# Token-side norm weights and wide splits of the turned banks in a four-layer float32 transformer on one Trainium2 core

## The reference, cut to what matters

```python
# first block, per layer
y = hybrid_mixer(x, ...)                       # in-projections, attention, gating, pooling, w_o
x = layer_norm(DN_ALPHA * x + y, ln1_g, ln1_b)
y = conv_gated_ffn(x, ...)                     # up, causal conv, silu gate, down
x = layer_norm(DN_ALPHA * x + y, ln2_g, ln2_b)
# second block, per layer
h = rmsnorm(x, norm_mix);  x = x + mixer2(h)   # delta rule, sparse attention, memory attention
h = rmsnorm(x, norm_ffn);  x = x + ffn2(h)
# at the end
return rmsnorm(x, norm_final)

layer_norm: (x - mean) * rsqrt(var + 1e-5) * g + b
rmsnorm:     x * rsqrt(mean(x * x) + 1e-6) * g
```

## Time and profile before

| | us |
|---|---|
| median of 3 runs | 2336.72 (2335.99 to 2337.41) |
| the profiled execution, its own time | 2335.5 |
| its span in the trace | 2333.4 |
| PE busy | 2182.3 (94%) |
| POOL busy | 1499.0 (64%) |
| ACT busy | 1072.1 (46%) |
| DVE busy | 938.7 (40%) |
| mean granted clock of PE | 0.961 of full |

### The profile page before, as it was taken

One profiled execution on the slowest core, in us unless ns is written; L12 is line 12 of the kernel. 1 busy time (PEld: TensorE's weight loads), 2 busy tenths in 40 slices (PEclk: granted clock), 3 DMA queues, 4 the chain that ended last, 5 costly groups with the idle time before them and its releaser, 6 DMA issues.

```text
span 2333.4 us, 35994 instructions
## 1 busy us (share of the span) xinstructions
PE 2182.3 (94%) x15336; PEld 2016.4 (86%) x15336; DVE 938.7 (40%) x1512; ACT 1072.1 (46%) x1511; POOL 1499.0 (64%) x632
## 2 busy tenths in 40 slices
PE   8999989899978989989999899899899899998997
PEld 7789977799868979879999899888789799998997
DVE  4342356422376546374112311456364561123113
ACT  4555555455545352345444444562522454544443
POOL 6688877698844233356778688662333566787885
PEclk9989999999979989999999999999989999999999
DMA  8345534355523122234445455342222344454553
GB/s 334 140 145 186 191 119 164 108 199 181 182 91 127 55 73 75 89 129 143 159 154 191 147 186 191 130 145 73 73 73 73 109 149 159 145 182 161 181 182 116
DMA packets 47183, 333.05 MB, mean 143 GB/s; under 512 B 5168, under 2 KB 5552, under 8 KB 7856
## 3 DMA queue, kind: packets, MB, share of 16 engines
q1 hardware_dynamic: 47024, 330.76, 41.0%
HBM read 329.69 MB, written 1.05 MB: 142 GB/s over the span
## 4 chain that ended last, share of the span: by engine, by line
PE 60%; DVE 8%; ACT 3%; issue 2%; POOL 0%; ACTq 0%; DVEq 0%
PE bank L146 14%; PE bank L148 13%; PE bank L147 13%; PE y L146 2%; PE y L148 2%; PE y L147 2%; PE bank L1679 2%; PE bank L1689 1%; DVE conv L1325 1%; PE bank L1612 1%; PE bank L1688 1%; DVE sc L2288 1%; PE bank L1734 1%; PE bank L1731 1%; PE bank L1507 1%
## 5 line engine op out<-in xcount | busy, mean ns | idle before, releaser
L336 POOL TENSOR_TENSOR w_lo<-w_raw,w_hi 128x1024 fp32r<-128x1024 f32 x602 | 1465.4, 2439 | 809.6 <-ACT w_hi L327 809.4
L327 ACT ACTIVATE w_hi<-w_raw 128x1024 fp32r<-128x1024 f32 x602 | 636.3, 1059 | 1055.5 <-PE bank L148 885.2
L146 PE MATMUL bank<-x_hi,w_hi 128*128 128x256 f32 x2960 | 881.0, 298 | 30.4 <-POOL w_lo L336 19.2
L147 PE MATMUL bank<-x_lo,w_hi 128*128 128x256 f32 x2960 | 851.8, 288 | 0.0
L148 PE MATMUL bank<-x_hi,w_lo 128*128 128x256 f32 x2960 | 851.6, 288 | 0.0
L146 PEld LDWEIGHTS bank<-x_hi,w_hi 128*128 128x128 f32 x2960 | 582.0, 197 | 57.1 <-issue 25.9
L147 PEld LDWEIGHTS bank<-x_lo,w_hi 128*128 128x128 f32 x2960 | 582.3, 197 | 10.6 <-issue 8.6
L148 PEld LDWEIGHTS bank<-x_hi,w_lo 128*128 128x128 f32 x2960 | 582.0, 197 | 0.0
L862 DVE SCALAR_TENSOR_TENSOR conv<-bank,par_sb,conv 128x254 f32<-128x254 f32 (+1 forms) x176 | 76.8, 478 | 255.0 <-ACT conv L850 253.5
L1188 DVE TENSOR_TENSOR hid_lo<-hid,hid_hi 128x512 fp32r<-128x512 f32 x22 | 44.8, 2038 | 246.7 <-ACT hid_hi L1183 246.7
L146 PE MATMUL y<-w_hi,hid_hi 128*128 128x512 f32 x352 | 139.2, 396 | 1.0 <-DVE hid_lo L884 1.0
...
## 6 DMA issues: line engine op xcount, KB each, us to landing
...
```

Source lines behind the costliest of these rows:

```text
L146: pe.matmul(out, lhs[0], rhs[0], start=start, stop=False, skip_group_check=skip)
L147: pe.matmul(out, lhs[0], rhs[1], start=False, stop=False, skip_group_check=skip)
L327: act.activation(self.hi[:, h % HALVES, :], self.raw[:, n % RAWS, i * HW:(i + 1) * HW], ACT.Copy).then_inc(*sig.up("high", h))
L336: pool.tensor_tensor(self.lo[:, h % HALVES, :], self.raw[:, n % RAWS, i * HW:(i + 1) * HW], self.hi[:, h % HALVES, :].bitcast(F32), ALU.su ...
```

## The change

It changes how the norms are computed and where their pieces stand in the queues.

- `Norm1` works in place on x_tok with the rows of weight and bias: `centred` = (x - mean) * weight, `scaled` = that * (1/sd) + bias, two scalar_tensor_tensor instructions with both tensor inputs in SBUF, instead of xn. For (0,1) ACT writes (x - mean)/sd and POOL applies the rows. PE turns x_tok itself, in the order (0,0), (1,0), (0,1), (1,1). The token copy needs no more work on POOL.
- A turned bank is split wide: ACT copies 128x512 from PSUM to x_hi (`high_parts`), DVE subtracts (`low_part`, 128x512).
- `Norm2` takes the squares' sums on ACT (Square with an accumulator), adds two 128x1 numbers on DVE, and writes xn = x_tok * (1/rms) * weight row in one instruction. Token tile 0 goes through to its end before tile 1's residual. The weight rows are loaded by five DMAs. The second `ln2` is folded into the first `norm_mix`.
- ACT's root of token tile 0 and the table load stand ahead of the weight halves +2 to +4, no longer behind them; POOL's queue follows.
- The feed-forward stages start in banks 4 and 5 instead of 0 and 1, and end in down8, down9, down10 behind val10.
- `Stream.by_tokens` and the branches on `self.split` are new, but nothing calls `by_tokens`, so the halves ahead of a norm are multiplied in the order of before.

```diff
 class Norm1:
     def pe(self, pe):
         net.main.pe(pe, self.end())
-        for tt in range(TT):
-            for k in range(KD):
-                if k % 4 == 0:
-                    pe.wait_ge(*sig.at("xn", *k_l, tt, k // 4))
+        for tt, half in ((0, 0), (1, 0), (0, 1), (1, 1)):
+            pe.wait_ge(*(sig.at("x_rest", *k_l) if (tt, half) == (0, 1) else sig.at("x_new", *k_l, tt, half)))
+            for k in range(4 * half, 4 * half + 4):
                 mm = pe.transpose(...)
     def act(self, act):
-        net.main.act(act, self.end())
...
+        main.act(act, self.end() - 6)
+        act.preload_act_table_set("sqrt_and_others")
+        root(0)
+        act.wait_ge(*sig.at("inverse", *k_l))
+        act.activation(net.xn[:, 0, HALF:D], net.xtok[:, 0, HALF:D], ACT.Identity, scale=net.rs[:, 0:1], bias=net.sd[:, 0:1]
+                       ).then_inc(*sig.up("xn_second", *k_l))
+        main.act(act, self.end())
+        root(1)
+        high_parts(net, act, k_l, self.tb)
     def dve(self, dve):
...
+        statistics(0)
+        dve.wait_ge(*sig.at("ln_rows_" + self.key, self.l))
+        centred(0, 0)
+        inverse(0)
...
+        scaled(0, 0)
+        statistics(1)
+        centred(1, 0)
+        inverse(1)
+        scaled(1, 0)
+        centred(1, 1)
+        low_part(net, dve, k_l, self.tb, 0)
+        scaled(1, 1)
+        for i in (1, 2, 3):
+            low_part(net, dve, k_l, self.tb, i)
     def pool(self, pool):
+        net.main.pool(pool, self.end() - 6)
...
+        net.pool_chain.step(pool.tensor_tensor(net.xtok[:, 0, c], net.xn[:, 0, c], rows[:, 0, c], ALU.mult))
+        pool.tensor_tensor(net.xtok[:, 0, c], net.xtok[:, 0, c], rows[:, 1, c], ALU.add).then_inc(*sig.up("x_rest", *k_l))
         net.main.pool(pool, self.end())

+def high_parts(net, act, k_l, tb):
+    for i in range(4):
+        act.wait_ge(*net.sig.at("turned_x", *k_l, i))
+        act.activation(net.xs[0][:, 2 * i:2 * i + 2, :], tb[i][:, :].rearrange("p (k t) -> p k t", k=2), ACT.Copy
+                       ).then_inc(*net.sig.up("x_turned_high", *k_l, i))
+
+def low_part(net, dve, k_l, tb, i):
+    c = slice(2 * i, 2 * i + 2)
+    dve.wait_ge(*net.sig.at("x_turned_high", *k_l, i))
+    dve.tensor_tensor(net.xs[1][:, c, :], tb[i][:, :].rearrange("p (k t) -> p k t", k=2), net.xs[0][:, c, :].bitcast(F32),
+                      ALU.subtract).then_inc(*net.sig.up("x_low", *k_l, i))

 class Norm2:
     def act(self, act):
+        main.act(act, self.end() - 6)
+        act.preload_act_table_set("sqrt_and_others")
+        if self.before is None:
+            squares(0)
+            root(0)
+            main.act(act, self.end())
+        else:
+            root_before(0)
+            main.act(act, self.end() - 2)
+            squares(0)
+            main.act(act, self.end())
+            root_before(1)
+            root(0)
+        squares(1)
+        root(1)
     def dve(self, dve):
+        def scaled(tt):
+            dve.wait_ge(*sig.at("x_squared", *k_l, tt, 1))
+            dve.tensor_tensor(net.ms[:, tt:tt + 1], net.bn[:, tt, 0, 0:1], net.bn[:, tt, 1, 0:1], ALU.add
+                              ).then_inc(*sig.up("square", *k_l, tt))
+            dve.wait_ge(*sig.at("root", *k_l, tt))
+            step(dve.reciprocal(net.rs[:, tt:tt + 1], net.sd[:, tt:tt + 1]))
...
+                dve.scalar_tensor_tensor(self.xn[:, tt, c], net.xtok[:, tt, c], net.rs[:, tt:tt + 1], net.mem2["gain"][:, c],
+                                         ALU.mult, ALU.mult).then_inc(*sig.up("xn", *k_l, tt, half))
+        if self.before is None:
+            residual(0)
+            scaled(0)
+            residual(1)
+            scaled(1)
+        else:
+            normed_before(0)
+            normed_before(1)
+            scaled(0)
+            scaled(1)

 class Feed1, Feed2:
-            if i:
+            if 0 < i < 9:
                 self.units.append(self.add_down(i - 1))
-        self.units.append(self.add_down(10))
+        for i in (8, 9, 10):
+            self.units.append(self.add_down(i))
```

More of the change, by code:

```diff
@@ L368, in pe @@
         sig = self.sig
[L369 to L370 removed]
+        for p in range(self.at_pe, min(pos, len(self.parts))):
+            h, part = self.parts[p]
             n, i, u, j = self.halves[h]
@@ L975, in dve, with statistics @@
         step = net.dve_chain.step
-        net.main.dve(dve, self.end())
-        for tt in range(TT):
+        rows = net.ln_rows[self.key]
+        def statistics(tt):
             for half in range(2):
@@ L1086, in act @@
     def act(self, act):
-        net, sig, k_l = self.net, self.net.sig, (self.key, self.l)
-        if self.after is not None:
-            net.main.act(act, self.end())
-        for tt in range(TT):
-            act.wait_ge(*sig.at("var", *k_l, tt))
-            act.activation(net.sd[:, tt:tt + 1], net.ms[:, tt:tt + 1], ACT.Sqrt).then_inc(*sig.up("root", *k_l, tt))
-        if self.key == "final":
-            return
-        if self.l == 0 and self.key == "norm_mix":
-            act.wait_ge(*sig.at("par2_loaded"))
@@ L1107, in dve, with added, residual @@
         step = net.dve_chain.step
-        if self.after is not None:
-            net.main.dve(dve, self.end())
+        def added(tt, half):
+            if tt == TT - 1 and half == 1:
+                dve.wait_ge(*sig.at("product", self.after().last))
+            else:
+                dve.wait_ge(*sig.at("summed", self.more, tt, half))
+            return net.y[:, tt * D + half * HALF:tt * D + (half + 1) * HALF]
+        def residual(tt):
+            for half in range(2):
+                c = slice(half * HALF, (half + 1) * HALF)
+                y = added(tt, half)
+                dve.tensor_tensor(net.xtok[:, tt, c], net.xtok[:, tt, c], y, ALU.add).then_inc(*sig.up("x_new", *k_l, tt, half))
@@ L2492, in chunk2, with gain_dram @@
         return self.a["w2"][l:l + 1, :, c].rearrange("o p n -> (o p) n")
+    def gain_dram(self, key, l):
+        i = 2 * DEPTH if key == "final" else 2 * l + ("norm_mix", "norm_ffn").index(key)
+        return self.a["gains"][i:i + 1, :]
     def ln_dram(self, l, key):
```

346 lines of the change are left out of this document (184 added, 162 removed).

## The result

| | changed kernel | kernel before |
|---|---|---|
| median of 5 runs, us | 2350.19 (2344.70 to 2351.56) | 2335.99 (2335.43 to 2337.41) |
| ratio | 1.0056, 95% interval 1.0044 to 1.0067 | |
| span of the profiled execution | 2348.4 | 2333.4 |
| mean granted clock of PE | 0.959 | 0.961 |

By the ratio the changed kernel is slower by 0.56%, and the interval leaves out 1; the two medians lie 14.2 us apart. The forecast was 2357.0 in a range of 2340 to 2366.

The account below looks back on a forecast made before the run. PE's matmul stream was taken to bound the kernel, the norms being breaks whose end DVE sets. Terms 20.4 + 7.0 - 0.4 - 3.3 - 3.6 - 1.0 + 1.2 = +20.3 us on 2336.7 gave 2357.0, range 2340 to 2366.

Parts of the forecast that it names:

- Collisions in Norm1: Three Norm1: DVE's tile 1 instructions wait for POOL's w_lo; stream starts at 18.7 against 11.9, 20.4 us later in three.
- POOL has its two x_rest operations first: In Norm1, POOL makes x_rest to 7.8, then w_lo +2, +3, +4 of 2.4 us each without a break.
- Collisions in Norm2: Three Norm2 before a stream: DVE waits for POOL's w_lo; stream at 14.0 against 11.7, 7.0 us later in three.
- ln2 with norm_mix: Second ln2 with norm_mix: some DVE instructions meet w_lo, yet the stream starts at 22.9 against 23.3, 0.4 us earlier.
- final: Final norm: no weight halves behind it, steps end at 8.3 instead of 11.6, 3.3 us gained.
- POOL's stalls: Behind Norm1, POOL loses six of eight token-copy operations; PE's w_lo waits of 1.81 us in both layers go, 3.6 gained.
- hid_lo: Feed-forward end: three held units behind val10 cover PE's hid_lo waits, 1.0 us gained.
- The positions' DMA: At norm_mix it waits for the turns; costed at nothing, covered by the wide splits, up to 1 us without them.
- PE's clock: Seven stream starts after norms: half clock loses 6.3 us instead of 5.1, so 1.2 lost; ends 5.1 gained, 7.5 lost.
- (a): At the norms DVE and POOL slip past each other without collision: -10.6 us, 2326.1, faster; chance 0.13.
- (b): Each norm meets only one or two w_lo, half of the collisions: +4.9 us, 2341.6; chance 0.19.
- (c): Forecast with the clock after norms at its bad end, 7.5 instead of 1.2: 2363.3; within the forecast's 0.68.
- (d): Clock stays up at every stream start, -5.1 instead of +1.2, all else as forecast: 2350.7; within the forecast's 0.68.

Follow-up runs that it names:

- e2: Changed kernel with POOL's w_lo +2 to +4 behind DVE's last two-tensor instruction at each norm, x_rest operations ahead of them: 2324.2 us, ratio 0.9958.
- e1: Changed kernel with POOL's two x_rest operations ahead of its w_lo +2 to +4 at each Norm1: 2344.1 us, ratio 1.0041.
- b2: Kernel before without POOL's adding of the bias to the token copy: 2329.8 us, ratio 0.9979.
- e5: Changed kernel with the positions' DMA issued about 180 us earlier, into a place of its own: 2345.9 us, ratio 1.0048.
- b1: Kernel before with POOL's token-copy pairs spread wider, two w_lo between pairs instead of one: 2344.5 us, ratio 1.0040.

## Why the prediction held, point by point

- **Collisions in Norm1 (+20.4 forecast, +21.7 measured).** The mechanism and its size were right, as e2 shows: with POOL's three halves behind DVE's last piece the stream starts at 13.5, the prediction's unblocked 13.7. The step that failed is "POOL has its two x_rest operations first"; it cost 0.6 us a norm. It rests on `Norm1.pool`, whose first line asks for the stream only up to half +1; but Mixer1 and Feed1 ahead of it had put all of POOL's halves up to +4 into the queue already. So POOL's x_rest came last, and PE waited for it (13.3 us in three). e1 shows that the working was right for the order it assumed. The size stayed the same because DVE and POOL finish the same sum of work in turns: the last of them ends at 128.6 or 129.7.
- **Collisions in Norm2 (+7.0, +6.6), ln2 with norm_mix (-0.4, -0.4), final (-3.3, -3.2).** Right within 0.3 us where the prediction named an end: xn(1,1) at t = 12.3 for 12.5 at `norm_ffn`, scaled(0,1) at 10.2 for 10.5 at `ln2` with `norm_mix`. The tiny sum of 2.08 us was included.
- **POOL's stalls (-3.6) and hid_lo (-1.0).** The waits went, but the term was mis-sized: each stall was followed by a drop of the clock, 1.6 us more (b2: 189.27 instead of 192.64 for a wait of 1.81). Both Feed1 together gave 9.4 instead of 4.6; the 6.6 of b2 and the 1.0 for hid_lo make 7.6 of it, and the rest is open. The second Mixer1 gave 3.0 that the sum did not have: waits of 0.7 for ACT's pooled and 0.3 for DVE's aqk are gone, and 3.4 us at half clock behind a wait of 1.95, though that wait is there in both. b1 and b2 show the first of these to be tied to the token operations; the clock's part was not tried apart, and in b2 it went the other way.
- **The positions' DMA (0, +1.1).** "DVE needs it only behind the splits" was true, but the DMA, issued at 649.07 in the kernel before for a CAST at 660.09, is now issued 2.85 us ahead of the CAST, and the splits that were named as its cover end at 668.06, 1.0 us too soon. e5 measured 1.1 us, just over the "up to 1 us" that stood as the price without cover.
- **PE's clock (+1.2).** The part at the starts of the streams is within its bounds but mis-sized: in the first 10 us of the seven streams 19.7 us ran at half clock, 13.0 before, and at the prediction's own 0.4 us that is 2.7 lost and not 1.2. It grew at the starts that had none before (4.4 and 1.6 us in the two Feed2, 3.8 in the second Mixer2, 1.5 in the second Mixer1) and shrank at the others. The larger part was not in the sum at all: Mixer2 with +7.6 and -6.9. That these nearly cancel in this trace is luck, and the changed kernel's times spread over 7 us. The range took it in by its width; no term of the sum stood for it.
- **Rivals.** (a), no collision, is out by the rows of 2.5 to 2.8 us; (b), half of the collisions, comes about as near to the median as the forecast (2341.6 and 2357.0 against 2350.2), but by the trace DVE was held up by all three w_lo, and by line 1070 as well. (c), the clock at its bad end, and (d), the clock up at every start, fall with the 19.7 us at half clock: (d)'s 2350.7 lies nearer to the measured median than the forecast does, but its condition did not hold at any of the seven starts.
